# Two TensorE quarters of a stick-breaking tick change places

## What is computed

```python
z = jnp.einsum('bhqd,bhkd->bhqk', qb, kb) * scale
mask = s_idx[None, :] < t_idx[:, None]
log_beta = jax.nn.log_sigmoid(z)
log_1m = jnp.where(mask, log_beta - z, 0.0)
log_a = log_beta + lax.cumsum(log_1m, axis=3, reverse=True) - log_1m
A = jnp.where(mask, jnp.exp(log_a), 0.0)
outs.append(jnp.einsum('bhqk,bhkd->bhqd', A, vb))
```

```python
sa = jnp.einsum('bhvk,bhk->bhv', S, -kk_t)
S = (S * w_t[:, :, None, :] + sa[..., None] * (kk_t * a_t)[:, :, None, :]
     + v_t[..., None] * k_t[:, :, None, :])
return S, jnp.einsum('bhvk,bhk->bhv', S, r_t)
```

## Time and profile before

| what | value |
|---|---|
| runs of the kernel, median of 3 | 1601.86 us (1601.29 to 1606.88) |
| the profiled execution, its own time | 1601.25 us |
| its span, first to last instruction | 1599.5 us |
| mixing stage in the span | about 363 to 784 us |
| TensorE busy, share of the span | 95% |
| VectorE, ScalarE busy, share of the span | 63%, 46% |
| mean granted TensorE clock | 0.986 |

### The profile page before, as it was taken

One profiled execution on the slowest core, in us unless ns is written; L12 is line 12 of the kernel. 1 busy time (PEld: TensorE's weight loads), 2 busy tenths in 40 slices (PEclk: granted clock), 3 DMA queues, 4 the chain that ended last, 5 costly groups with the idle time before them and its releaser, 6 DMA issues. The chain is left out here.

```text
span 1599.5 us, 37215 instructions
## 1 busy us (share of the span) xinstructions
PE 1526.3 (95%) x15568; PEld 1281.8 (80%) x15568; DVE 1008.8 (63%) x1582; ACT 737.9 (46%) x1302; POOL 168.9 (11%) x225
## 2 busy tenths in 40 slices
PE   6999999997999999999699989999999999999997
PEld 6999999996777777777478868888888888888886
DVE  6142434426988888788766785555555766667666
ACT  6253534435877787777645453333333111110132
POOL 6132434321011010110000000000000000000000
PEclk9999999997999999999999999999999999999999
DMA  4334362555523332220434454233332322223235
GB/s 173 137 120 166 133 219 97 201 186 152 133 50 67 75 83 59 50 50 13 129 83 132 158 178 158 105 106 108 115 120 103 125 93 89 92 98 106 92 106 184
DMA packets 89964, 185.76 MB, mean 116 GB/s; under 512 B 7744, under 2 KB 48192, under 8 KB 89552
## 3 DMA queue, kind: packets, MB, share of 16 engines
q1 hardware_dynamic: 86064, 169.68, 34.0%
q10 hardware_dynamic: 3744, 13.85, 2.2%
HBM read 124.96 MB, written 57.49 MB: 114 GB/s over the span
## 5 line engine op out<-in xcount | busy, mean ns | idle before, releaser
L534 DVE TENSOR_TENSOR inproj_wl<-xn_raw,inproj_wh 128x1024 fp32r<-128x1024 f32 x27 | 33.0, 1222 | 150.5 <-ACT inproj_wh L425 150.5
L638 PE MATMUL inproj_acc<-xn_xh,inproj_wh 128*128 128x348 f32 (+1 forms) x384 | 126.5, 329 | 0.0
L638 PE MATMUL inproj_acc<-xn_xl,inproj_wh 128*128 128x348 f32 (+1 forms) x384 | 123.4, 321 | 0.0
L638 PE MATMUL inproj_acc<-xn_xh,inproj_wl 128*128 128x348 f32 (+1 forms) x384 | 123.3, 321 | 0.0
L2276 DVE TENSOR_TENSOR all_mh_f<-all_mh_f,tail_bank 128x512 f32<-128x512 f32 x112 | 76.7, 685 | 52.3 <-PE tail_bank L2430 50.5
L2276 DVE TENSOR_TENSOR all_ml_f<-all_ml_f,tail_bank 128x512 f32<-128x512 f32 x112 | 76.7, 685 | 52.0 <-PE tail_bank L2430 52.0
L2430 PE MATMUL tail_bank<-all_ml,tail_th 128*128 128x512 f32 x256 | 100.9, 394 | 0.0
L2430 PE MATMUL tail_bank<-all_mh,tail_tl 128*128 128x512 f32 x256 | 100.9, 394 | 0.0
L2430 PE MATMUL tail_bank<-all_mh,tail_th 128*128 128x512 f32 x256 | 100.9, 394 | 0.0
L2430 PE MATMUL tail_bank<-tail_th 128*128 128x512 f32 x256 | 99.8, 390 | 0.3 <-DVE tail_tl L2177 0.3
L2430 PE MATMUL tail_bank<-tail_tl,tail_th 128*128 128x512 f32 x256 | 99.8, 390 | 0.0
(11 more groups left out here) (323 smaller groups left out, 4371.3 us busy)
## 6 DMA issues: line engine op xcount, KB each, us to landing
tail_raw<-in_w_up SPq DMA_DIRECT2D x32, 512.0 KB, 4.5
u_scratch<-tail_c SPq DMA_DIRECT2D x64, 256.0 KB, 2.1
tail_raw_d<-in_w_down SPq DMA_DIRECT2D x32, 512.0 KB, 3.6
tail_raw_u<-u_scratch SPq DMA_DIRECT2D x32, 512.0 KB, 3.3
xn_raw<-in_w_in SPq DMA_DIRECT2D x28, 512.0 KB, 5.0
p_scratch<-inproj_out ACTq DMA_DIRECT2D x26, 520.0 KB, 2.7
chunk_scratch<-inproj_fields SPq DMA_DIRECT2D x4, 2720.0 KB, 9.5
mix_swp<-chunk_scratch SPq DMA_DIRECT2D x34, 256.0 KB, 5.0
```

What stands on the lines that cost most here:

```text
L534: w_low.done(dve.tensor_tensor(wl[s][:, :, :], raw[s][:, :, :], wh[s][:, :, :].bitcast(F32), ALU.subtract), "all")
L638: last = pe.matmul(acc[g][:, 0:size], w[s][:, kt, :], xx[:, kt, col:col + size], start=(kt == 0 and j == 0), stop=(kt == KD - 1 and j == 2))
```

## The change

In TensorE's list of a tick, the first two quarters change places: `z` (or the turn) of task `now` now stands in the first quarter, and `tri` of task `now - 4` in the second. Third and fourth quarter stay. No instruction is added or removed, and the lists of ScalarE, VectorE, GpSimd and the DMA queues stay as they are.

```diff
                 for now in range(N + SB_LAG + 1):
-                    t = now - 4
-                    if is_task(t):
-                        soft_low.wait(pe, t)
-                        if at(t).first:
-                            exponent.wait(pe, t - 2)
-                        sums(tri, tri_r, t, at(t).first).then_inc(tri_done.sem, 1)
-                    yield
                     t = now
                     if at(t) is not None:
                         z_copied.wait(pe, t - 1)
...
                         last.then_inc(z_done.sem, 1)
+                    yield
+                    t = now - 4
+                    if is_task(t):
+                        soft_low.wait(pe, t)
+                        if at(t).first:
+                            exponent.wait(pe, t - 2)
+                        sums(tri, tri_r, t, at(t).first).then_inc(tri_done.sem, 1)
                     yield
                     t = now - 5
```

## The result

The change makes the kernel slower by a fifth of a per cent. The median of 20 runs is 1606.28 us, beside 1602.43 us for 20 runs of the kernel before; the ratio on record is 1.002, with a 95% interval of 1.0011 to 1.0028. Worked out from the ratio, the loss is 3.2 us (1.8 to 4.5); between the two medians lie 3.9 us. Further down, a loss in us beside a ratio is always worked out from the ratio. The forecast was 1605.6 us. Of all executions named here one was in a slower state (1885.17 us at a mean granted clock of 0.749, in e5_copy_first), and its ratio leaves it out; the median there without it is 1602.32.

The account below looks back on a forecast made before the run. TensorE was taken to set the mixing stage's pace, VectorE a close second. Copy waits of 4.8 us less 0.5 us for the low half made 4.3 us on 1601.25, so 1605.6 us; range 1599.5 to 1613.

Parts of the forecast that it names:

- Second step, the copy: Mixing stage: TensorE's z waits for ScalarE's copy of the task before; 7.1 us at 15 listed places, 4.8 us net.
- the deductions: Taken off the 7.1 us of copy waits: 0.7 for z coming earlier, 1.1 for neighbouring places, 0.9 for waits absorbed.
- First step: ScalarE's copy waits less for z, 24.8 us falling to 8 to 12; worth 0 to TensorE, at most 2.3 us.
- Rival B: ScalarE, freed of about 16 us of waiting, runs ahead where copies were late; 0 to 1.5 us remain; chance 0.22.
- Third step: TensorE's tri, a quarter later, waits less for VectorE's low half: 0.5 us off, between 0 and 1.1.
- Fourth step: VectorE's exponent waits more for tri, 4.7 us in 14 ticks; taken as 0 for TensorE.
- The sum: Whole kernel: 4.8 - 0.5 = 4.3 us on the profiled execution's 1601.25 us, so 1605.6 us.
- the forecast's own sign: In the profile after, TensorE's z waits for ScalarE's copy some 4 to 7 us at 8 to 17 places.
- Rival E: New waits bring two more drops of TensorE's clock, 3.4 us on top of the sum: 1609 us; chance 0.03.
- C: VectorE's exponent waits for tri, making scan copies late for TensorE; 4.7 us on top, 1610.3 or 1613.5 us; chance 0.16.
- D: TensorE's waits for scan copies go, 8.7 us faster: 1592.6 us; chance 0.04.
- The low end of the range: Whole kernel: 1599.5 us, where ScalarE's lead gives back its 2.3 us.

Follow-up runs that it names:

- e5_copy_first: The change, plus ScalarE's copy of z moved to its first quarter, ahead of the exponential of the weights; 1602.75 us, ratio 0.9996 against the kernel before.
- e1: Kernel before with the two quarters swapped only in the 36 ticks that a scan part cuts between first and second quarter; 1605.67 us, ratio 1.0035.
- e3: Kernel before with z, then tri, both in TensorE's first quarter, second quarter empty; 1607.59 us, ratio 1.0043.
- e6: Kernel before, quarters swapped only in the 19 scan-cut ticks with no value product between the two z; 1607.23 us, ratio 1.0027.
- e2: Kernel before with the two quarters swapped only in the 96 ticks that no scan part cuts between them; 1601.12 us, ratio 1.0001.
- e4: Kernel before with TensorE's first quarter empty, and z, then tri, in the second; 1600.32 us, ratio 0.9994.
- e7: Kernel before, quarters swapped only in the 13 scan-cut ticks with a value product between the two z; 1602.13 us, ratio 0.9998.
- e9: Kernel before with z, then tri, in TensorE's first quarter, and ScalarE's copy of z in its first quarter; 1602.82 us, ratio 1.0011.
- e8: Kernel before with ScalarE's list alone changed: copy of z in the first quarter, exponential of the weights in the second; 1607.73 us, ratio 1.0042.

## Why the prediction was right

**The bound.** TensorE sets the pace of the stage. That held: every run with long waits of TensorE for the copy was slower (8.1 to 12.7 us of weight loads: the change and its repetition, e1, e3, e6), and of the runs without them e2, e4, e5 and e7 were not, and e9 not beyond its interval. e8 was slower, and there TensorE waits for other copies of ScalarE.

**Second step, the copy.** It was the step with the forecast in it: 4.8 us, from 15 places. In the trace after, the distance from the end of a copy to the start of the next `z` is 0.05 us wherever TensorE waited, and this is so in 15 ticks behind the turns at the start. Thirteen are places of the list, those at tasks 88 and 115 didn't come, and tasks 62 (one of the two without `tri`) and 99 did. By how much later `z` starts there than the usual 0.23 us behind the product before it, they add up to 5.8 us, the largest at tasks 8 and 60, 0.72 us each; 0.2 us of it, at task 32, were there before. The same measure in the other traces, beside the loss:

| run | places | `z` later by | loss by the ratio |
|---|---|---|---|
| the change | 15 | 5.8 us | 3.2 us (1.8 to 4.5) |
| e10, the change again | 16 | 5.8 us | 5.1 us (2.7 to 7.4) |
| e1 | 15 | 5.4 us | 5.6 us (3.4 to 8.0) |
| e6 | 16 | 6.9 us | 4.3 us (2.2 to 6.4) |
| e3 | 17 | 10.3 us | 6.9 us (4.3 to 9.3) |
| e2, e4, e5, e7, e9 | 1 to 3 | under 0.5 us | none clear of zero |

So the loss goes with this delay and is in most rows a part of it; how much of it is absorbed, these intervals don't tell. Of the deductions the first was right: task 49 shrank from 0.33 to 0.02 us and task 34 from 0.43 to 0.19, and the waits at 88 and 115 are gone, since all four copies had themselves waited for `z`. The second was not right everywhere: tasks 8 and 9 fell together from 1.67 to 1.24 us, but 60 and 61 rose from 0.78 to 1.07. And task 62 alone has 0.60 us, where 0.4 were added for 62 and 87.

**First step, ScalarE.** Its waits for `z` fell to 11.9 us, as forecast (8 to 12). That such a fall gives nothing back is shown by e2, to within 2 us. In the profile after, VectorE's clamp L1230 is ScalarE's next wait, 24.2 us. (Rival B takes the 16 waits that were to go for 16 us; from 24.8 to 11.9 it is 12.9 us.)

**Third step, the low half.** The wait of `tri`'s weight loads for L1223, 1.1 us in the kernel before, is no longer among the waits after. What it is worth in time, 0.5 us by the forecast, is too small for any run here.

**Fourth step, VectorE.** In this execution its waits for `tri` grew to 9.3 us, where 5 to 8 were forecast. In e10, another execution of the same program, they are 6.9 us in the same stretch, and in e5, where TensorE waits for no copy, 7.5. So the surplus isn't shown to belong to the change, nor to TensorE's new waits. What these waits cost TensorE was taken as nothing, and e4, with 12.2 us of them in the whole stage, bears it out.

**The sum.** 4.3 us were forecast; the ratio gives 3.2 (1.8 to 4.5), and in the repetition 5.1 (2.7 to 7.4). The forecast lies within both intervals, but they are wide. The waits for the copy were forecast as 5.7 us before the 0.9 us for what is absorbed, beside the 5.8 us counted above; how much is absorbed no run measures. That the whole sum comes so near is in part luck. In the forecast's own sign, TensorE was to wait for the copy 4 to 7 us at 8 to 17 places: over the whole stage its products wait 4.0 us, 8 times, and its weight loads 8.5 us, 15 times, the lower end and more than the upper one. The profiled execution took 5.3 us longer than that of before, and its stage 6.2. Part of the 6.2 is the clock. Behind the place at task 74 TensorE ran for 6.7 us at a granted clock of 0.50, 1.2 GHz; in the kernel before it was 3.4 us, so 1.7 us come from there (half of the added 3.4):

```profile
603.00:607.30 4.30, 1.75 (x32) 1.04 (x30) 3.17 (x7) 2.47 (x5) 0.54 (x2) 1.00 0.43 80
607.30:614.00 6.70, 6.35 (x100) 4.82 (x104) 4.40 (x9) 2.75 (x6) 0.83 (x3) 0.50 0.01 2
```

That is not a law of the change: in e10, the same program, this stretch was 3.4 us, and that at 481 us was missing. It doesn't make the whole execution longer either, for the tail of the kernel before has a stretch of 3.4 us at 0.50 (from 955.9 us) that the change's doesn't have. Rival E falls with the granted clocks of all executions: their mean is 0.987 for the change (20 executions) and again for its repetition (11), and 0.985 to 0.986 for the three sets of the kernel before (30, 29 and 22). The slower program had, if anything, the higher clock. In Perfetto Trace Analysis, section Matmul Optimizations, the Trainium skill says that the engine scales its power with its use. The new gaps here are under 0.8 us, and the two traces of the change show no drop in common that the kernel before lacks.

**The rivals.** B (it cancels) left 0 to 1.5 us and fell with the ratio's interval, and with the 15 places, C with e3 and e4, and D with the sign of the change. The low end of the range, 1599.5, is reckoned from the median 1601.86, not from the 1601.25 of the sum; from there it would be 1599.0.

## What to carry to other kernels

When two engines hand one buffer to and fro in a static order, look at the phase of both lists. Here the copy had to follow its product with no scan part between them, and the next product needed more TensorE work between it and the last than ScalarE had ahead of its copy. Moving one engine's step by a quarter without the other's turned slack into waits, and such a wait is found beforehand from the old trace, by laying the new start beside the end of the step that frees the buffer. Only waits of the engine that sets the pace entered the sum: 12.2 us of waiting on VectorE brought no loss here, while 8 to 10 us of waits of TensorE's weight loads (5.4 to 6.9 us by the starts of `z`) came with losses of 3 to 6.

## What the runs showed that I had not expected

ScalarE, busy for 78% of the middle of the stage, could bear to wait 26 us for `z`, but not 62: then 12.4 us of TensorE's weight loads waited for its scan copies, and 6.7 us were lost. The slack of an engine that isn't the bound has an end; where it lies between 26 and 62 us, no run tells. And two executions of one program differ in how long TensorE's clock is at its lower level: behind 395 us in the stage the change has 10.2 us of it in one trace, with a span of 1604.8 us, and 3.4 us in the other (e10), with a span of 1601.8. Half of that difference, 3.4 us, is about what the spans differ by (3.0 us). Among the traces of all programs here it goes from none (e1) to 13.6 us (e6), so a single profiled span is no measure of a change of this size.
